# Even layer of a two-block network: bias rows behind the chunk loop, 64-column weights in the chunk steps, LRU work in small pieces

## What is computed

```
proj = xn @ w_in
log_a = -8 * sigmoid(gate_a) * softplus(-lambda);  a = exp(log_a)
u = sqrt(-expm1(2*log_a)) * sigmoid(gate_x) * conv(lru_x)
h_t = a_t * h_(t-1) + u_t                      # 512 channels
y_lru = gelu(lru_g) * h
S_t = S * w_t - (S kk_t) (kk_t a_t)^T + v_t k_t^T   # 8 heads of 64 x 64
o_t = S_t r_t
y_rwkv = (group_norm(o) + bonus) * g
x = x + concat(y_lru, y_rwkv) @ w_out
```

## Time and profile before

| | |
|---|---|
| three executions | 2059.86, 2060.0, 2068.55 us; median 2060.0 |
| span of the profiled execution | 2053.0 us, 25736 instructions |
| its own time beside the span | not listed apart; the median lies 7.0 us above the span |
| TensorE busy | 1911.3 us (93%) |
| VectorE busy | 1560.9 us (76%) |
| ScalarE busy | 1163.7 us (57%) |
| mean granted clock of TensorE | 0.932 |
| chain that ended last | PE 73%, DVE 10%, issue 10%, ACT 4%, DMA 2% |

### The profile page before, as it was taken

The page is one execution under the profiler, slowest core; times in us unless marked ns, Lnnn a source line. Parts: engine busy times, 40 slices in busy tenths (PEclk is TensorE's granted clock), DMA queues, the critical chain, the costliest instruction groups (busy, mean ns, idle before and its releaser), DMA issues.

```text
span 2053.0 us, 25736 instructions
## 1 busy us (share of the span) xinstructions
PE 1911.3 (93%) x9348; PEld 1608.3 (78%) x9348; DVE 1560.9 (76%) x1530; ACT 1163.7 (57%) x1218; POOL 59.8 (3%) x85
## 2 busy tenths in 40 slices
PE   7989879999977899999999999999999989888987
PEld 7988767887855788888888888888888877777766
DVE  6873566888675788888888889988888876656754
ACT  6632034434454667766766766767766855545542
POOL 1000001110110000000000000000000000000000
PEclk9997589999977899999999999999999999969978
DMA  6300138997421699999999999999999954213420
GB/s 219 123 1 31 35 109 288 328 327 245 144 92 42 233 373 349 363 372 340 372 348 362 346 360 378 334 373 347 363 371 338 372 209 149 83 42 126 142 79 21
DMA packets 161948, 489.03 MB, mean 238 GB/s; under 512 B 8178, under 2 KB 13427, under 8 KB 161744
## 3 DMA queue, kind: packets, MB, share of 16 engines
q1 hardware_dynamic: 153536, 458.21, 61.7%
q0 software_dynamic: 8336, 29.81, 4.1%
HBM read 485.36 MB, written 2.62 MB: 238 GB/s over the span
## 4 chain that ended last, share of the span: by engine, by line
PE 73%; DVE 10%; issue 10%; ACT 4%; DMA 2%; POOL 0%; DVEq 0%; ACTq 0%; POOLq 0%
PE bank L1139 20%; PE bank L1140 20%; PE bank L1141 20%; DVE weights_at L1888 2%; PE bank L1374 2%; PE bank L1622 2%; PE bank L1348 1%; PE bank L1687 1%; ACT weights_at L2798 1%; PE bank L1336 1%; PE bank L1362 1%; DMA BIG<-in_e_ffn_gate 1%; PE bank L1425 1%; DMA BIG<-in_e_ffn_down 1%; DVE x_low L1915 1%
## 5 line engine op out<-in xcount | busy, mean ns | idle before, releaser
L2456 DVE TENSOR_TENSOR expert_weights_low<-BIG,expert_weights_high 128x2048 fp32r<-128x2048 f32 x336 | 750.2, 2287 | 55.1 <-ACT expert_weights_high L3076 55.0
L3076 ACT ACTIVATE expert_weights_high<-BIG 128x2048 fp32r<-128x2048 f32 x336 | 625.3, 1922 | 63.1 <-DMA BIG<-in_o_moe_up 36.7
L1139 PE MATMUL bank<-expert_weights_high,expert_x_high 128*128 128x512 f32 x896 | 351.5, 392 | 2.9 <-DVE expert_x_low L2521 2.8
L1141 PE MATMUL bank<-expert_weights_low,expert_x_high 128*128 128x512 f32 x896 | 349.0, 389 | 0.0
L1140 PE MATMUL bank<-expert_weights_high,expert_x_low 128*128 128x512 f32 x896 | 348.8, 389 | 0.0
L1888 DVE TENSOR_TENSOR weights_at<-BIG,weights_at 128x2048 fp32r<-128x2048 f32 (+2 forms) x100 | 219.1, 2191 | 85.4 <-ACT weights_at L2798 83.0
L2798 ACT ACTIVATE weights_at<-BIG 128x2048 fp32r<-128x2048 f32 (+2 forms) x100 | 183.6, 1836 | 165.9 <-DMA BIG<-in_e_ffn_down 38.0
L1139 PE MATMUL bank<-weights_at,x_high 128*128 128x512 f32 (+2 forms) x608 | 244.5, 402 | 24.0 <-DVE weights_at L1888 10.3
L1140 PE MATMUL bank<-weights_at,x_low 128*128 128x512 f32 (+2 forms) x608 | 239.1, 393 | 0.0
L1141 PE MATMUL bank<-weights_at,x_high 128*128 128x512 f32 (+2 forms) x608 | 238.8, 393 | 0.0
L1139 PEld LDWEIGHTS bank<-expert_weights_high,expert_x_high 128*128 128x128 f32 x896 | 168.3, 188 | 37.3 <-DVE expert_x_low L2521 3.0
(11 more groups left out here) (398 smaller groups left out, 2407.0 us busy)
## 6 DMA issues: line engine op xcount, KB each, us to landing
BIG<-in_o_moe_gate SPq DMA_DIRECT2D x112, 1024.0 KB, 5.1
BIG<-in_o_moe_up SPq DMA_DIRECT2D x112, 1024.0 KB, 5.2
BIG<-in_o_moe_down SPq DMA_DIRECT2D x112, 1024.0 KB, 5.1
BIG<-in_w_ada POOLq DMA_DIRECT2D x48, 512.0 KB, 5.0
BIG<-in_w_in SPq DMA_DIRECT2D x20, 1024.0 KB, 5.0
BIG<-in_o_w_qkv SPq DMA_DIRECT2D x12, 1024.0 KB, 5.1
BIG<-in_e_w_in SPq DMA_DIRECT2D x10, 1024.0 KB, 5.2
BIG<-in_e_ffn_gate SPq DMA_DIRECT2D x10, 1024.0 KB, 5.4
```

Source lines behind the costliest of these rows:

```text
L1139: mm(b, high_l, high_r, start=start, stop=False, skip_group_check=not check)
L1141: last = mm(b, high_l, low_r, start=False, stop=stop, skip_group_check=not check)
L2456: tt_(E_WL[q % E_SLOTS], half(q % E_SLOTS), E_WH[q % E_SLOTS].bitcast(F32), SUB).then_inc(w_low, 1)
L3076: f(E_WH[q % E_SLOTS], half(q % E_SLOTS), ACT.Copy).then_inc(w_high, 1)
```

## The change

The bias matmuls and their copies move behind the chunk loop on TensorE, ScalarE and in the plan of banks. On ScalarE five heads are copied ahead of the root of the group norm's variance and three behind it. In Z, SA and O the weights are the 64 columns of the chunk's own tokens instead of 128, and they write the chunk's own 64 partitions of the bank; dS stays. `fill` stands ahead of the waits for operands. The LRU's VectorE work is cut: the reciprocal into quarters, the two products apart, the scans and the gate into step 3. `low(2)` moves ahead of the loop.

```diff
@@ -204,8 +204,6 @@
             add(("dY", s, g), "v")
             if s < LEVELS[-1]:
                 add(("dX", s, g), "v")
-    for h in range(NE):
-        add(("bias", h), "a")
     for tt in range(TT):
         add(("ZV", tt), "a")
         add(("OV", tt), "a")
@@ -216,6 +214,8 @@
         if c < 3:
             add(("dS", c), "v")
         add(("O", c), "a")
+    for h in range(NE):
+        add(("bias", h), "a")
     for u in range(2):
         add(("OT", u), "v")
     row("w_out", 0)
@@ -1349,12 +1349,6 @@
                                       start=True, stop=True)
                         last.then_inc(filled, 1)
 
-            for h in range(NE):
-                b = fill(pe, ("bias", h))
-                mm(b[:, 0:BIAS_ROW], s_relb[0:32, h:h + 1].broadcast_to([32, P]), BUCK[0:32, :],
-                   start=True, stop=True).then_inc(filled, 1)
-
-
             for tt in range(TT):
                 for name, w in (("ZV", 0), ("OV", 1)):
                     b = fill(pe, (name, tt))
@@ -1366,31 +1360,38 @@
 
             for c in range(4):
                 tt, r = c // 2, slice(64 * (c % 2), 64 * (c % 2) + 64)
-                t0 = slice(tt * P, (tt + 1) * P)
-
-                def group(name, parts):
-                    b = fill(pe, name)
+                own = slice(c * HALF, (c + 1) * HALF)
+
+                def group(b, rows, parts):
                     for i, (c0, n, lhs, rhs) in enumerate(parts):
-                        last = mm(b[:, c0:c0 + n], lhs, rhs, start=i == 0, stop=i == len(parts) - 1,
+                        last = mm(b[rows, c0:c0 + n], lhs, rhs, start=i == 0, stop=i == len(parts) - 1,
                                   skip_group_check=True)
                     last.then_inc(filled, 1)
 
-                state = lambda w: [(p * P, P, QR[:, p, w, t0], ST[c % 2][:, p, :]) for p in range(4)] if c else []
+                state = lambda w: [(p * P, P, QR[:, p, w, own], ST[c % 2][:, p, :]) for p in range(4)] if c else []
                 if c:
+                    b = fill(pe, ("Z", c))
                     pe.wait_ge(state_ready, c)
-                    group(("Z", c), state(0))
+                    group(b, r, state(0))
+                    b = fill(pe, ("SA", c))
                     wait_taken(pe, ("Z", c))
                 else:
+                    b = fill(pe, ("SA", c))
                     wait_taken(pe, ("ZV", 0))
                 z = ZS if c else ZVAL[:, 0, :]
-                group(("SA", c), [(h * 64, 64, YI[r, at_head(tt, h), :], z[r, h * 64:h * 64 + 64])
-                                  for h in range(8)])
+                group(b, r, [(h * 64, 64, YI[r, at_head(tt, h), r], z[r, h * 64:h * 64 + 64]) for h in range(8)])
+                b = fill(pe, ("dS" if c < 3 else "O", c))
                 wait_taken(pe, ("SA", c))
                 if c < 3:
-                    group(("dS", c), [(p * P, P, a[r, tt, p * P:(p + 1) * P], b_[r, p * P:(p + 1) * P])
-                                      for p in range(4) for a, b_ in ((TMK, SAN), (TMT, TMV[:, tt, :]))])
-                group(("O", c), state(1)
-                      + [(h * 64, 64, B1T[r, at_head(tt, h), :], SAN[r, h * 64:h * 64 + 64]) for h in range(8)])
+                    group(b, slice(0, P), [(p * P, P, a[r, tt, p * P:(p + 1) * P], b_[r, p * P:(p + 1) * P])
+                                           for p in range(4) for a, b_ in ((TMK, SAN), (TMT, TMV[:, tt, :]))])
+                    b = fill(pe, ("O", c))
+                group(b, r, state(1) + [(h * 64, 64, B1T[r, at_head(tt, h), r], SAN[r, h * 64:h * 64 + 64])
+                                        for h in range(8)])
+            for h in range(NE):
+                b = fill(pe, ("bias", h))
+                mm(b[:, 0:BIAS_ROW], s_relb[0:32, h:h + 1].broadcast_to([32, P]), BUCK[0:32, :],
+                   start=True, stop=True).then_inc(filled, 1)
             pe.wait_ge(gn_ready, 1)
             to_channels(("OT",), 2, lambda u: [(P, (2 * j + m) * P, OO[:, m, (2 * u + j) * P:(2 * u + j + 1) * P])
                                                for j in range(2) for m in range(TT)])
@@ -2086,15 +2087,24 @@
                 for c in range(4):
                     V(ts(T1[:, c, :], GA[:, c, :], s_l[5][:, c:c + 1], None, MUL), decay_arg if c == 3 else None)
 
+            def lru_denominator():
+                v.wait_ge(decay_ready, 1)
+                V(ts(T1, T2, 1.0, None, ADD))
+
             def lru_reciprocal(i):
-                V(d.reciprocal(T1[:, 2 * i:2 * i + 2, :], T1[:, 2 * i:2 * i + 2, :]))
-
-            def lru_scan():
+                V(d.reciprocal(T1[:, i, :], T1[:, i, :]))
+
+            def lru_root_argument():
+                V(stt(T2, T2, 2.0, T1, MUL, MUL), root_arg)
+
+            def lru_input(by):
                 v.wait_ge(root_ready, 1)
-                V(tt_(T2, T2, GX, MUL))
-                V(tt_(T2, T2, XC, MUL))
-                for c in range(4):
-                    V(d.tensor_tensor_scan(T1[:, c, :], GA[:, c, :], T2[:, c, :], 0.0, MUL, ADD))
+                V(tt_(T2, T2, by, MUL))
+
+            def lru_scan(c):
+                V(d.tensor_tensor_scan(T1[:, c, :], GA[:, c, :], T2[:, c, :], 0.0, MUL, ADD))
+
+            def lru_gated():
                 V(tt_(YT[:, 0:4, :], T1, LG, MUL), lru_done)
 
 
@@ -2130,13 +2140,23 @@
                         join(LEVELS[n + 1], gr)
 
             lru_decay()
+            low(2)
             for c in range(4):
                 r = slice(64 * (c % 2), 64 * (c % 2) + 64)
                 if c:
                     b = take(v, ("Z", c))
                     wait_taken(v, ("ZV", c // 2))
                     V(tt_(ZS[r, :], b[r, :], ZVAL[r, c // 2, :], ADD), ev)
+                if c == 1:
+                    lru_reciprocal(0)
+                elif c == 2:
+                    lru_root_argument()
+                elif c == 3:
+                    lru_input(XC)
                 V(ts(SAN[r, :], take(v, ("SA", c))[r, :], -1.0, None, MUL), ev)
+                if c == 1:
+                    lru_reciprocal(1)
+                    lru_reciprocal(2)
                 if c < 3:
                     b = take(v, ("dS", c)).rearrange("p (h t) -> p h t", h=4)
                     V(tt_(DS, b, bc(cst("same_head"), 1, [P, 4, P]), MUL), ev)
@@ -2144,17 +2164,16 @@
                         V(tt_(DS, DS, ST[c % 2], ADD))
                     V(tt_(ST[(c + 1) % 2], DS, bc(s_pl[:, :, c], 2, [P, 4, P]), MUL), state_ready)
                 if c == 0:
-                    v.wait_ge(decay_ready, 1)
-                    V(ts(T1, T2, 1.0, None, ADD))
-                    lru_reciprocal(0)
+                    lru_denominator()
                 elif c == 1:
-                    lru_reciprocal(1)
-                    V(stt(T2, T2, 2.0, T1, MUL, MUL), root_arg)
+                    lru_reciprocal(3)
                 elif c == 2:
-                    lru_scan()
+                    lru_input(GX)
                 elif c == 3:
+                    for i in range(4):
+                        lru_scan(i)
+                    lru_gated()
                     lambda_difference()
-                    low(2)
 
             wait_taken(v, ("O", 3))
             V(tt_(OO, OO, OVAL, ADD))
@@ -2895,9 +2914,6 @@
                 for gr in range(4):
                     b = take(act, ("U", s, gr)).rearrange("p (h t) -> p h t", h=4)
                     A(f(UU[:, 4 * gr:4 * gr + 4, :], b, ACT.Copy), ea)
-            for h in range(NE):
-                A(f(ROWB[h // 4][:, h % 4, :], take(act, ("bias", h))[:, 0:BIAS_ROW], ACT.Copy),
-                  ea)
             for tt in range(TT):
                 A(f(ZVAL[:, tt, :], take(act, ("ZV", tt)), ACT.Copy), ea)
                 A(f(OVAL[:, tt, :], take(act, ("OV", tt)), ACT.Copy), ea)
@@ -2909,9 +2925,17 @@
                 A(f(OO[r, c // 2, :], take(act, ("O", c))[r, :], ACT.Copy), ea)
                 if c == 1:
                     root(1, root_arg, root_ready, T2)
+
+            def bias_rows(heads):
+
+                for h in heads:
+                    A(f(ROWB[h // 4][:, h % 4, :], take(act, ("bias", h))[:, 0:BIAS_ROW], ACT.Copy), ea)
+
             act.wait_ge(lru_done, 1)
             A(f(XTH[:, 0:4, :], YT[:, 0:4, :], ACT.Copy), x_high)
+            bias_rows(range(5))
             root(1, gn_var, gn_root, s_var)
+            bias_rows(range(5, NE))
             act.wait_ge(yT_ready, 1)
             A(f(XTH[:, 4:8, :], YT[:, 4:8, :], ACT.Copy), x_high)
             high(2)
```

## The result

The changed kernel takes 2029.57 us in the median of four executions (2027.17 to 2030.75), against 2060.58 for the kernel before, measured again beside it: a ratio of 0.9845, with a 95% interval from 0.9823 to 0.9866. That is 31 us less.

What follows compares the result with a forecast made beforehand. The prediction took the TensorE and VectorE chain from dY to OT as the bound; 7.1 + 3.4 + 12.1 + 2.0 + 1.3, less 0.2, gave 25.7 us saved and 2034.5 us, range 2026 to 2048.

Steps and rivals of the forecast that it cites:

- The bound: From dY to OT TensorE and VectorE alternate without slack or transfer waits; a microsecond saved there is one at the end.
- Bias rows leave the front: Ahead of ZV and OV: 16 bias matmul instructions stood alone on the chain; removing them saves 7.1 us.
- ZV and OV move into fuller clock: Right behind dY: 3.5 us at full clock, then half; 10.4 us instead of 13.85, 3.4 less (bounds 0 and 6.9).
- The clock holds: Rival: ZV, OV and parts of the loop stay at full clock; 3.4 more, up to 10 in the loop, 2021; chance 0.08.
- 64-column weights: Solves and O's head parts in the chunk loop: load time halves, 1.7 us a group, 12.1 us for seven; state pairs nothing.
- narrow weights save nothing: Rival in the chunk loop: 64-column loads go no faster, so the 12.1 us goes; 2047.5 us, chance 0.12.
- their loads don't overlap: Rival in the chunk loop: narrow loads no longer overlap the running matmul, about 0.47 us a pair; 2087 us, chance 0.04.
- Mode changes: Where 64-row and 128-row weights meet, loads pause 0.22 us; new changes in the loop cost at most +0.4 us.
- LRU work in pieces: VectorE's cut work fits its waits in the chunk loop: 2.0 us saved in step 0, 1.3 in step 2.
- Bias rows in the tail: Between O(3) and OT: bias matmuls take 10.24 us in a 10.32 us window, +0.2 us on OT (bounds -2, +3).
- The base: Whole kernel: span 2053.0 us, with the median of 2060.0 lying 7.0 above it, added back to the forecast span.
- The signs: Expected: clock falling 3.5 us in, solves about 2.0, loop 45, no ZS wait; wrong if bias, not norm, ends OT.

Runs made afterwards that it cites:

- the control: The kernel before, run again with no edit: 2057.12 us, a ratio of 0.9996 [0.9983, 1.0009].

## Why the prediction was right, and where it was not

**The bound.** Right. The stretch was TensorE and VectorE in turn, and what was saved in it arrived.

**Bias rows leave the front.** Right, 7.1 us.

**ZV and OV move into fuller clock.** This is the step that failed, by half of its size: 6.8 us came, not 3.4. I had reasoned that work which doesn't bring the clock up doesn't hold it up either. The runs refute that: ZV and OV went 14 us at 1.2 GHz without a rise where they began low, and 7.1 us at 2.4 GHz without a fall where they began high, in all ten profiles that start them behind dY. I had named 6.9 as the bound. It is the first half of the rival "The clock holds"; my argument against that one, that the clock had never risen in this work, says nothing about a clock that is already up. The same clock reached into step 0, where the first solve and part of dS gave 2.2 us more than forecast. These two are the whole difference between 25.5 and 31.2. The clock fell all the same, 10.6 us behind dY; what made it fall there no run isolates.

**64-column weights.** Right. A solve's loads go at 1.78/16 = 0.111 us each at 1.2 GHz, where I had taken 0.108. The state's pairs, put at no gain, load 64 columns behind 128 streamed ones at 1.56/8 = 0.195 us (the second line below): there the streamed columns set the pace, as I had argued for the 96-column row. Undoing the narrow weights costs 13.1 to 13.8 us, of which I had 12.1 in the sum and 1.7 more in step 0's. The rival that narrow weights save nothing and the one that their loads don't overlap are both out.

The weight loads in the changed kernel, to be set against the earlier trace rows:

```profile
193.70 1.78 PEld L1367 LDWEIGHTS bank<-BIG 64*64 64x64 f32 x16 [1.31 <-issue]
...
200.30 1.56 PEld L1367 LDWEIGHTS bank<-BIG 128*64 128x64 f32 x8 [0.23 <-issue]
202.19 3.46 PEld L1367 LDWEIGHTS bank<-BIG 64*64 64x64 f32 x24 [0.33 <-issue]
```

The Trainium skill, TensorE: Matmul & The Clock Gate, "LDWEIGHTS (loading the stationary operand)", has the load's time go with its columns; these runs agree (0.111 for 64 columns where it was 0.216 for 128).

**Mode changes.** Right in size. The weight loads pause 0.22 to 0.33 us at each change of shape. Inside a group that is on the chain, but there were pauses of 0.22 before, and steps 1 to 3 came out as summed without a term for it.

**LRU work in pieces.** Right for the whole. Steps 1 to 3 came out within 0.1 us of the sum, and the two terms, 2.0 and 1.3, together with the 12.1 of the weights are what came. The split between weights and pieces is not. The prediction did not say how the two lean on each other: the pieces are worth 1.9 us with wide weights and 6.3 to 7.0 with narrow ones, where I had put 3.3, and the narrow weights are worth 8.6 in the loop without the pieces.

**Bias rows in the tail.** Right in size, 0.1 us against 0.2. But OT comes at the bias rows' end and not at the norm's, which I had named as a sign of being wrong: they took 10.6 us, not 10.2, and the norm ended 0.2 us ahead of OT. As a sign it was too strict, for a bias that ends last by so little costs no more than that.

**The base.** Wrong: I put 7.0 us outside the span, and it is 1.8. The profile shown was of an execution of about 2054.8 us, 5 below the median. In the sum the two cancel, since I added the same 7.0 back.

**The signs.** Solves took 1.94 us (about 2.0 forecast), and no VectorE work held up ZS in step 2. From the first solve to the end of O(3) it was 42.5 us, not 45, and the clock fell 10.6 us behind dY, not 3.5.

## What to carry to other kernels

Ask at which clock a moved piece will start, and not only at which it ran: the same matmuls kept 2.4 GHz when they came right behind dense work and stayed at 1.2 when they came behind the bias rows. Cut VectorE's work to the size of TensorE's waits together with shortening TensorE's groups; either alone gave 1.9 and 8.6 us in the loop, and the two undone one by one cost 6.3 and 13. Filler work belongs where an engine waits for something long, and as filler it should be checked for becoming the last to end, as the bias rows are by 0.1 to 0.2 us and as the eight idle matmuls in the tail were by 1.

## What the hardware showed that was not expected

- The same matmuls kept whichever clock they began with: 64 pairs of 128x128 weights with 64 streamed columns went 14 us at 1.2 GHz without a rise and 7.1 us at 2.4 GHz without a fall.
- The clock differed with the rows of the array in use, at the same streamed columns. The bias matmuls over 32 rows fell from 2.4 GHz after 3.5 us in the earlier trace rows and after 4.2 in the control, and stayed at 1.2 GHz for all of their 10.6 us in the tail of the changed kernel, both times it was profiled. Over 128 rows, most of them zeros, the clock rose 2.8 us into them, and they took 6.8 us; with idle matmuls behind them it rose after 5.6 us, and they took 8.2.
- Idle float32 matmuls of 0.43 us each in the waits of 0.9 us carried the clock further: one in each wait until 17.9 us behind dY, two until 24.6, where without them it fell after 10.6 to 11.8.
- Executions of one kernel on one chip spread over 10 us (2053.6 to 2064.3, the kernel before), and its feed-forward layer alone took 212.6 and 216.9 us in two profiles; a single profile's span is no base for a forecast to the microsecond.
